# Stage boundaries with repeated reciprocals as weights, halved weight slots, and layer-norm squares added on VectorE

## The chip, the core and the metric

The kernel runs on one core of one Trainium2 chip. The metric is the device time of one execution in microseconds. Engines: TensorE (PE; its weight loads stand apart as PEld), VectorE (DVE), ScalarE (ACT), GpSimd (POOL), and SyncE (SP), which issues the transfers.

## What is computed

A trunk of two layers on x of 512 tokens and 1024 channels, float32. Each layer is a SwiGLU feed-forward block (inner width 2816) with weight 1/2, a mixer, and a second such block; every block normalises its input and its output:

```python
f = swiglu(rms_norm(h, norm_pre[i, 0]), w_ffn_in[i, 0], w_ffn_out[i, 0])
h = h + FFN_RES_WEIGHT * rms_norm(f, norm_post[i, 0])
t = rms_norm(h, norm_pre[i, 1])
...                                    # layer 0: attention; layer 1: convolution module
h = h + rms_norm(t, norm_post[i, 1])
f = swiglu(rms_norm(h, norm_pre[i, 2]), w_ffn_in[i, 1], w_ffn_out[i, 1])
h = h + FFN_RES_WEIGHT * rms_norm(f, norm_post[i, 2])

def rms_norm(x, g):
    return x * rsqrt(mean(x * x) + 1e-6) * g

def conformer_conv_module(h, ...):
    a = h @ w_pw1 + b_pw1
    u = a[..., :CONV_CH] * sigmoid(a[..., CONV_CH:])
    y = causal depthwise convolution of u, width 31, + b_dw
    mu = mean(y); var = mean((y - mu) ** 2)          # layer_norm over channels
    y = silu((y - mu) * rsqrt(var + 1e-5) * ln_g + ln_b)
    return y @ w_pw2 + b_pw2
```

## The kernel before

Everything is held transposed: channels on the 128 partitions in eight chunks, tokens on the free axis. Weights come as a stream of slots, 128 x 1024 float32 each (eight 128x128 blocks, or six for the last group of a feed-forward block), into a ring of four (`raw`). For precision each slot is split: ScalarE copies it to `w_hi` (line 745), VectorE subtracts to get `w_lo` (line 970), and each block product is three passes, hi x hi, lo x hi, hi x lo (lines 360 to 362). Slot n + 4 is split once slot n has been multiplied; its raw data was loaded by SyncE when the slot before it in the ring place had been split.

There are six sub-layers (`sub` 0 to 5). Each ends in `down`, which leaves the output f in SBUF, chunk by chunk, squares it on ScalarE and adds the squares on VectorE. The last slot of it is computed in two halves of 256 tokens (`last_slot`). Then comes the boundary. TensorE's `post_stat` sums the squares over the channels as one column of four per-token-block values (`add_columns`, line 377), ScalarE takes the root (line 757), VectorE inverts it to `r_col`, 128 x 4 (line 975), and multiplies it onto four diagonals (line 976); TensorE spreads it over all partitions with a product of ones and the diagonals (`broadcast`, line 383). Fillers (`keep_warm`, line 371) stand before and after it. VectorE then normalises f from that bank and adds the residual (lines 1069, 1074), ScalarE makes x_hi of the next sub-layer (line 749), and its first body starts (`four_slots`, line 399). The last ring place's slot is split within the boundary: ScalarE behind the root, VectorE behind the diagonals. A second inversion and spread, for the norm before the sub-layer, stands within the first body, which `r_pre` (line 762) keeps. The sixth boundary ends in `output`: TensorE adds four residual chunks (line 500) and products with the gains (line 509), VectorE the rest.

In the convolution (sub 4) TensorE runs sixteen bodies of the first projection (two for each chunk of channels), and between them `convolve(j)` (line 656) on groups of channels with their taps on a matrix that VectorE builds (line 1214). The input u of it goes through DRAM: VectorE's gate, a store (line 273) and a load in another layout (line 279), both queued on SyncE. Results are biased and centred on VectorE (lines 1226, 1232) and squared on ScalarE (line 900); the sums over channels are products with `same_q` on TensorE (line 664; 4 products of 128x128, which float32 makes eight passes). Those of the values are `sum_rest`, those of the squares `sum_squares`. The order of each engine's work is written out by hand in the code, and semaphores join them. VectorE's first step on the variance is line 1281.

## Time and profile before

| | us |
|---|---|
| median of 3 runs | 1902.97 (1902.47 to 1903.03) |
| the profiled execution | 1901.29 |
| its span | 1899.4 |
| TensorE busy | 1878.8 (99%) |
| VectorE busy | 1009.5 (53%) |
| ScalarE busy | 634.0 (33%) |

Starts in the timeline are microseconds from the span's start. A float32 or float32r product shows one row for each pass. The duration of a matmul is longer than the distance to the next, because they are pipelined: a 512-column pass lasts 0.39 and the next starts 0.23 later.

### The profile page before, as it was taken

Reading aid. Unit: us, or ns where it says so; the run is one execution under the profiler, and the core shown is the slowest. Engines: PE = TensorE matmul, PEld = TensorE weight load, DVE = VectorE, ACT = ScalarE, POOL = GpSimd, SP = SyncE. Lnnn points to the kernel's source line nnn. Section 1 sums busy time; section 2 is a strip of 40 time slices with the busy share of each in tenths; the row PEclk is TensorE's granted clock in tenths of the full one; section 3 lists DMA queues with packets and bytes.
Section 4 is the critical chain, followed back from the end, with each engine's and each line's share of the span. In section 5 each row is a group of like instructions: output and inputs, shape, how many; then the busy total and the mean of one; then the engine's idle time right before and its main releaser. Section 6 shows DMA issues by size and latency. Waiting matters only on the chain.

```text
span 1899.4 us, 24198 instructions
## 1 busy us (share of the span) xinstructions
PE 1878.8 (99%) x8969; PEld 1543.8 (81%) x8969; DVE 1009.5 (53%) x1377; ACT 634.0 (33%) x915; POOL 28.0 (1%) x54
## 2 busy tenths in 40 slices
PE   8999999999999999999999999999999999999998
PEld 6888888887688888888788888887998888888886
DVE  5534434688666434435754443457765674344345
ACT  5322322346634223223442232234112543222223
POOL 0000000021000000000000000000000000000000
PEclk9999999999999999999999999999999999999999
DMA  5333233321023332333233323332332223332331
GB/s 189 111 100 100 88 102 98 114 87 58 24 77 100 100 99 89 100 100 100 67 122 100 99 89 100 100 111 80 122 121 79 78 82 95 100 100 91 97 99 56
DMA packets 62096, 181.49 MB, mean 96 GB/s; under 512 B 7088, under 2 KB 16448, under 8 KB 62032
## 3 DMA queue, kind: packets, MB, share of 16 engines
q1 hardware_dynamic: 60432, 179.09, 29.7%
q0 software_dynamic: 1600, 1.51, 0.3%
q8 instruction: 44, 0.72, 0.2%
q14 instruction: 20, 0.16, 0.0%
HBM read 173.63 MB, written 6.29 MB: 95 GB/s over the span
## 4 chain that ended last, share of the span: by engine, by line
PE 96%; DVE 3%; ACT 1%; DMA 0%; issue 0%; SPq 0%; DVEq 0%; ACTq 0%
PE bank L360 27%; PE bank L362 27%; PE bank L361 27%; PE bank L656 3%; PE bank L399 2%; PE bank L400 2%; PE bank L403 2%; PE bank L377 1%; PE bank L605 1%; PE bank L589 1%; PE bank L664 1%; DVE w_lo L970 1%; PE bank L570 1%; ACT w_hi L745 0%; DVE h_resid L1074 0%; PE bank L546 0%
## 5 line engine op out<-in xcount | busy, mean ns | idle before, releaser
L970 DVE TENSOR_TENSOR w_lo<-w_raw,w_hi 128x1024 fp32r<-128x1024 f32 x312 | 381.5, 1225 | 447.5 <-ACT w_hi L745 436.8
L360 PE MATMUL bank<-x_hi,w_hi 128*128 128x512 f32 x1448 | 567.6, 392 | 0.8 <-DVE gate_tmp L1003 0.2
L362 PE MATMUL bank<-x_hi,w_lo 128*128 128x512 f32 x1448 | 563.5, 389 | 0.0
L361 PE MATMUL bank<-x_lo,w_hi 128*128 128x512 f32 x1448 | 563.4, 389 | 0.0
L745 ACT ACTIVATE w_hi<-w_raw 128x1024 fp32r<-128x1024 f32 x312 | 328.2, 1055 | 602.0 <-PE bank L362 600.0
L360 PE MATMUL bank<-a_hi,w_hi 128*128 128x512 f32 (+1 forms) x844 | 320.7, 380 | 0.4 <-DVE w_lo L970 0.4
L360 PEld LDWEIGHTS bank<-x_hi,w_hi 128*128 128x128 f32 x1448 | 271.9, 188 | 60.2 <-issue 2.6
L361 PE MATMUL bank<-a_lo,w_hi 128*128 128x512 f32 (+1 forms) x844 | 319.9, 379 | 0.0
L362 PE MATMUL bank<-a_hi,w_lo 128*128 128x512 f32 (+1 forms) x844 | 319.9, 379 | 0.0
L361 PEld LDWEIGHTS bank<-x_lo,w_hi 128*128 128x128 f32 x1448 | 271.9, 188 | 57.2 <-issue 1.4
L362 PEld LDWEIGHTS bank<-x_hi,w_lo 128*128 128x128 f32 x1448 | 271.9, 188 | 56.5
L360 PEld LDWEIGHTS bank<-a_hi,w_hi 128*128 128x128 f32 x844 | 158.8, 188 | 32.0 <-DVE a_lo L1015 1.0
L362 PEld LDWEIGHTS bank<-a_hi,w_lo 128*128 128x128 f32 x844 | 158.8, 188 | 29.8
L361 PEld LDWEIGHTS bank<-a_lo,w_hi 128*128 128x128 f32 x844 | 158.8, 188 | 29.7
L1003 DVE TENSOR_TENSOR up_tmp<-bank,r_pre 128x512 f32<-128x512 f32 x96 | 66.2, 690 | 191.7 <-PE bank L362 191.7
L776 ACT ACTIVATE a_hi<-up_tmp 128x512 f32 (+1 forms) x88 | 55.6, 632 | 276.6 <-DVE up_tmp L1013 276.6
L774 ACT ACTIVATE gate_tmp<-gate_tmp 128x512 f32<-128x512 f32 x88 | 55.7, 632 | 160.4 <-DVE gate_tmp L1003 160.4
L1015 DVE TENSOR_TENSOR a_lo<-up_tmp,a_hi 128x512 f32 (+1 forms) x88 | 60.9, 692 | 79.9 <-ACT a_hi L776 79.9
L399 PE MATMUL bank<-x_hi,w_hi 128*128 128x512 f32 x168 | 67.2, 400 | 9.0 <-DVE w_lo L1319 8.2
L1003 DVE TENSOR_TENSOR gate_tmp<-bank,r_pre 128x512 f32<-128x512 f32 x106 | 72.4, 683 | 0.0
L1013 DVE TENSOR_TENSOR up_tmp<-up_tmp,gate_tmp 128x512 f32<-128x512 f32 x88 | 60.9, 692 | 13.7 <-ACT gate_tmp L774 3.3
L400 PE MATMUL bank<-x_hi,w_lo 128*128 128x512 f32 x168 | 66.4, 395 | 0.0
(169 smaller groups left out, 1263.4 us busy)
## 6 DMA issues: line engine op xcount, KB each, us to landing
w_raw<-stream SPq DMA_DIRECT2D x312, 512.0 KB, 3.5
h_resid<-xT SPq DMA_DIRECT2D x8, 256.0 KB, 6.5
w_raw<-stream SPq DMA_DIRECT2D x8, 256.0 KB, 6.1
u_scratch<-V SPq DMA_DIRECT2D x8, 256.0 KB, 2.3
u_groups<-u_scratch SPq DMA_DIRECT2D x8, 256.0 KB, 2.7
qT<-z_scratch SPq DMA_DIRECT2D x8, 256.0 KB, 3.7
outT<-h_resid SPq DMA_DIRECT2D x8, 256.0 KB, 2.2
z_scratch<-kT SPq DMA_DIRECT2D x4, 256.0 KB, 2.5
```

The source lines that it names most:

```text
L360: nc.tensor.matmul(out, lw[0], lx[0], start=first, stop=False)
L361: nc.tensor.matmul(out, lw[0], lx[1], start=False, stop=False)
L362: return nc.tensor.matmul(out, lw[1], lx[0], start=False, stop=last)
L399: nc.tensor.matmul(bank[s][:, :], blk(w_hi, s, k), x[0][:, k, :], start=(k == 0), stop=False)
L400: nc.tensor.matmul(bank[s][:, :], blk(w_lo, s, k), x[0][:, k, :], start=False, stop=False)
L656: last = nc.tensor.matmul(bank[6 + j % 2][:, g * NT:(g + 1) * NT], mats[g][:, m, :, :].rearrange("p c q -> p (c q)"), ug[:, j % 2, g, m:m ...
L745: nc.scalar.activation(w_hi[:, s, :], raw[:, s, :], ACT.Copy).then_inc(s_hi, 1)
L774: nc.scalar.activation(g, g, ACT.Silu).then_inc(s_act, 1)
L970: nc.vector.tensor_tensor(w_lo[:, s, :], raw[:, s, :], w_hi[:, s, :].bitcast(F32), ALU.subtract).then_inc(s_lo, 1)
L1003: nc.vector.tensor_tensor(dst, bank[s][:, :], r_pre[:, :], ALU.mult).then_inc(s_evac, 1)
L1013: nc.vector.tensor_tensor(U[:, p, :], U[:, p, :], G[:, p, :], ALU.mult).then_inc(s_prod, 1)
L1015: nc.vector.tensor_tensor(a_lo[:, chunk, :], U[:, p, :], a_hi[:, chunk, :].bitcast(F32), ALU.subtract).then_inc(s_a, 1)
```

## The change

The diagonals are gone. `broadcast` multiplies with the column of `r_col`, repeated 128 times, as the weights, and the identity as the moving data, one product of 128x128 for each of four token blocks. Since it reads `ident`, the first spread waits for the constants. The fillers before it are three instead of six. In the last slot's turn both halves of the weights of the last ring place are split on their own: on ScalarE around the second square, ahead of the root; on VectorE one before the reciprocal, one after. The sum of the layer norm's squares is made by seven additions on VectorE, and TensorE sums one tile instead of eight.

```diff
             def broadcast():
-                return nc.tensor.matmul(BCAST[:, :], ones[:, :], sq[:, 0, :],
-                                        start=True, stop=True)
+                for t in range(NB):
+                    ins = nc.tensor.matmul(BCAST[:, t * P:(t + 1) * P], r_col[:, t:t + 1].broadcast_to([P, P]),
+                                           ident[:, :], start=True, stop=True)
+                return ins
...
                 else:
-                    keep_warm(6)
+                    keep_warm(3)
...
-                def sum_squares(j):
-                    if j == 0:
-                        pe.wait_ge(s_root, 2 * sub + 1)
-                    pe.wait_ge(s_zsq, j + 1)
-                    sum_groups(STAT, zsq[j % 3], j == 0, j == KD - 1).then_inc(s_sqmm, 1)
+                def sum_squares():
+                    pe.wait_ge(s_root, 2 * sub + 1)
+                    pe.wait_ge(s_zsqadd, KD - 1)
+                    sum_groups(STAT, zsq_sum, True, True).then_inc(s_sqmm, 1)
...
                         nc.scalar.activation(sq[:, m % 2, HALVES[0]], f[:, m, HALVES[0]], ACT.Square
                                              ).then_inc(s_fsq0, 1)
+                        if n + RING < SLOTS:
+                            act.wait_ge(s_raw[s], 16 * (n // RING) + 32)
+                            act.wait_ge(s_mm, n + 1)
+                            nc.scalar.activation(w_hi[:, s, W_HALVES[0]], raw[:, s, W_HALVES[0]], ACT.Copy
+                                                 ).then_inc(s_hi_half, 1)
                         act.wait_ge(s_evac, n + 1)
                         nc.scalar.activation(sq[:, m % 2, HALVES[1]], f[:, m, HALVES[1]], ACT.Square
                                              ).then_inc(s_fsq, 1)
+                        if n + RING < SLOTS:
+                            nc.scalar.activation(w_hi[:, s, W_HALVES[1]], raw[:, s, W_HALVES[1]], ACT.Copy
+                                                 ).then_inc(s_hi, 1)
...
-                link(nc.vector.reciprocal(r_col[:, :], root_col[:, :]))
-                nc.vector.tensor_tensor(diag, ident[:, None, :].broadcast_to([P, NB, P]),
-                                        r_col[:, :, None].broadcast_to([P, NB, P]), ALU.mult).then_inc(done, 1)
+            def inverse_of_roots(done):
+
+                nc.vector.reciprocal(r_col[:, :], root_col[:, :]).then_inc(done, 1)
...
+                def add_squares(j):
+                    dve.wait_ge(s_zsq, j + 1)
+                    if j >= 2:
+                        dve.wait_ge(s_zsqadd, j - 1)
+                    nc.vector.tensor_tensor(zsq_sum, zsq_sum, zsq[j % 2], ALU.add).then_inc(s_zsqadd, 1)
```

VectorE's queue at the boundary of sub 0. f_out<-bank3 is the last evacuation, w_lo the low half of a weight slot, f_out<-f_out,bank5 the first normalisation. Before:

```order
L1024 TENSOR_TENSOR f_out<-bank3,f_out 128x256
L975 RECIPROCAL r_col<-root_col 128x4
L976 TENSOR_TENSOR sq_tmp<-ident,r_col 128x512
L970 TENSOR_TENSOR w_lo<-w_raw,w_hi 128x1024
L1069 TENSOR_TENSOR f_out<-f_out,bank5 128x512
```

and in the changed kernel:

```order
L1034 TENSOR_TENSOR f_out<-bank3,f_out 128x256
L982 TENSOR_TENSOR w_lo<-w_raw,w_hi 128x512
L987 RECIPROCAL r_col<-root_col 128x4
L982 TENSOR_TENSOR w_lo<-w_raw,w_hi 128x512
L1083 TENSOR_TENSOR f_out<-f_out,bank5 128x512
```

The diagonals left the queue, and half of the weight slot stands before the reciprocal.

ScalarE's queue at the same place; sq_tmp are the squares, root_col the root, x_hi the next sub-layer's input. Before:

```order
L795 ACTIVATE sq_tmp<-f_out 128x256
L798 ACTIVATE sq_tmp<-f_out 128x256
L757 ACTIVATE root_col<-bank4,eps 128x4
L745 ACTIVATE w_hi<-w_raw 128x1024
L749 ACTIVATE x_hi<-h_resid,cols 128x512
```

and in the changed kernel:

```order
L795 ACTIVATE sq_tmp<-f_out 128x256
L800 ACTIVATE w_hi<-w_raw 128x512
L803 ACTIVATE sq_tmp<-f_out 128x256
L806 ACTIVATE w_hi<-w_raw 128x512
L757 ACTIVATE root_col<-bank4,eps 128x4
L749 ACTIVATE x_hi<-h_resid,cols 128x512
```

The slot's copy moved from behind the root to before it, in two parts.

TensorE's queue at the end of the convolution, from convolve(6) on: bank67 takes the convolution, bank5 the sums of the values, bank4 those of the squares. Before:

```order
L656 MATMUL bank67<-u_groups,f_out 128x128 x27
L656 MATMUL bank67<-u_groups,tap_matrix 128x128 x9
L664 MATMUL bank5<-kT,conv_consts 128x128 x8
L664 MATMUL bank4<-gate_tmp,conv_consts 128x128 x4
L664 MATMUL bank4<-up_tmp,conv_consts 128x128 x4
L664 MATMUL bank4<-sum_sq,conv_consts 128x128 x4
L656 MATMUL bank67<-u_groups,f_out 128x128 x27
L656 MATMUL bank67<-u_groups,tap_matrix 128x128 x9
L664 MATMUL bank5<-rope_cos,conv_consts 128x128 x4
L664 MATMUL bank5<-rope_sin,conv_consts 128x128 x4
L664 MATMUL bank4<-gate_tmp,conv_consts 128x128 x4
L664 MATMUL bank4<-up_tmp,conv_consts 128x128 x4
```

and in the changed kernel:

```order
L662 MATMUL bank67<-u_groups,f_out 128x128 x27
L662 MATMUL bank67<-u_groups,tap_matrix 128x128 x9
L670 MATMUL bank5<-kT,conv_consts 128x128 x8
L662 MATMUL bank67<-u_groups,f_out 128x128 x27
L662 MATMUL bank67<-u_groups,tap_matrix 128x128 x9
L670 MATMUL bank5<-rope_cos,conv_consts 128x128 x4
L670 MATMUL bank5<-rope_sin,conv_consts 128x128 x4
L670 MATMUL bank4<-gate_tmp,conv_consts 128x128 x4
```

Three of the sums of squares stood between the two convolutions and two at the end (three more before the last body); one is left, at the end. On VectorE the additions 1 and 2 stand ahead of the bias of group 6, 3 to 5 behind its centring, 6 and 7 behind that of group 7.

## Rows read from the trace of the kernel before

**Rows 1.** The page's part 4, the chain that ended last, by engine.

```profile
PE 96%; DVE 3%; ACT 1%; DMA 0%; issue 0%; SPq 0%; DVEq 0%; ACTq 0%
```

**Rows 2.** Timeline, all engines, boundary of sub 0: start us, us, engine, line, out<-in.

```profile
373.71 0.42 DVE L1024 TENSOR_TENSOR f_out<-bank,f_out 128x256 f32<-128x256 f32 x1 [0.60 <-PE bank L362]
374.17 0.42 ACT L798 ACTIVATE sq_tmp<-f_out 128x256 f32<-128x256 f32 x1 [1.68 <-DVE f_out L1024]
...
374.32 1.03 PE L377 MATMUL bank<-ones,sq_tmp 128*128 128x1 f32 x8
...
375.22 1.46 PE L371 MATMUL bank<-mask,ident_b 128*128 128x512 bf16 x6
375.39 0.26 ACT L757 ACTIVATE root_col<-bank,eps 128x4 f32<-128x4 f32 x1 [0.81 <-PE bank L377]
...
375.69 0.18 DVE L975 RECIPROCAL r_col<-root_col 128x4 f32<-128x4 f32 x1 [1.55 <-ACT root_col L757]
375.90 0.69 DVE L976 TENSOR_TENSOR sq_tmp<-ident,r_col 128x512 f32<-128x512 f32 x1
376.63 1.23 DVE L970 TENSOR_TENSOR w_lo<-w_raw,w_hi 128x1024 fp32r<-128x1024 f32 x1
...
376.65 1.12 PE L383 MATMUL bank<-sq_tmp,ones 128*128 128x512 f32 x2
...
377.61 2.32 PE L371 MATMUL bank<-mask,ident_b 128*128 128x512 bf16 x10
...
377.81 0.69 DVE L1069 TENSOR_TENSOR f_out<-f_out,bank 128x512 f32<-128x512 f32 x1
...
380.09 0.50 PE L399 MATMUL bank<-x_hi,w_hi 128*128 128x512 f32 x1 [0.16 <-ACT x_hi L749]
```

**Rows 3.** Timeline, TensorE, end of the convolution.

```profile
1429.14 1.06 PE L664 MATMUL bank<-gate_tmp,conv_consts 128*128 128x128 f32 x8
...
1437.28 6.19 PE L656 MATMUL bank<-u_groups,f_out 128*128 128x128 f32 x54
...
1445.31 1.95 PE L664 MATMUL bank<-kT,conv_consts 128*128 128x128 f32 x16
...
1449.78 6.19 PE L656 MATMUL bank<-u_groups,f_out 128*128 128x128 f32 x54
...
1461.38 1.06 PE L664 MATMUL bank<-up_tmp,conv_consts 128*128 128x128 f32 x8
```

**Rows 4.** Timeline, VectorE, end of the convolution.

```profile
1458.02 0.69 DVE L1226 TENSOR_TENSOR rope_sin<-bank,conv_consts 128x512 f32<-128x512 f32 x1 [9.27 <-PE bank L656]
...
1460.69 0.29 DVE L1276 TENSOR_SCALAR mean_rest<-bank 128x128 f32<-128x128 f32 x1 [1.25 <-PE bank L664]
...
1462.55 0.29 DVE L1281 SCALAR_TENSOR_TENSOR var<-bank,mean_early 128x128 f32<-128x128 f32 x1 [0.65 <-PE bank L664]
```

**Rows 5.** Groups by line: shapes, count, busy us, mean ns, idle before.

```profile
L1319 DVE TENSOR_TENSOR w_lo<-w_raw,w_hi 128x512 fp32r<-128x512 f32 x8 | 5.4, 692 | 1.9 <-ACT w_hi L939 1.9
...
L939 ACT ACTIVATE w_hi<-w_raw 128x512 fp32r<-128x512 f32 x8 | 5.0, 630 | 1.6 <-DMA w_raw<-stream 1.4
```

**Rows 6.** Timeline, TensorE, last boundary.

```profile
1885.06 1.10 PE L500 MATMUL bank<-h_resid,ident 128*128 128x512 f32 x2
1886.48 1.13 PE L383 MATMUL bank<-sq_tmp,ones 128*128 128x512 f32 x2 [0.32 <-DVE sq_tmp L976]
```

**Rows 7.** Timeline, SyncE's queue, and the landing of the transfer at 1445.70.

```profile
1442.47 0.32 SPq L273 DMA_DIRECT2D u_scratch<-V  x1
...
1445.70 0.37 SPq L279 DMA_DIRECT2D u_groups<-u_scratch  x1
...
DMA to landing us min/median/max: 2.8/2.8/2.8
```

**Rows 8.** Timeline, TensorE, the program's first passes.

```profile
11.76 1.91 PE L403 MATMUL bank<-x_lo,w_hi 128*128 128x512 f32 x4
...
15.41 1.07 PE L403 MATMUL bank<-x_lo,w_hi 128*128 128x512 f32 x4
```

More of the change, by code:

```diff
@@ L148, in build_program @@
         zg = [z.rearrange("p (g n) -> p g n", g=GROUPS) for z in (kf[:, 0:T], kf[:, T:2 * T], rc[:, :], rs[:, :])]
-        zsq = [z.rearrange("p (g n) -> p g n", g=GROUPS) for z in (G[:, 0, :], U[:, 0, :], ss[:, :])]
+        zsq_sum, *zsq = [z.rearrange("p (g n) -> p g n", g=GROUPS) for z in (G[:, 0, :], U[:, 0, :], ss[:, :])]
         m0, dl, var = sb("mean_early", [P, NT]), sb("mean_rest", [P, NT]), sb("var", [P, NT])
@@ L422, in spread @@
                 def spread():
+                    if sub == 0:
+                        pe.wait_ge(s_const, CONSTS)
                     pe.wait_ge(s_diag, 2 * sub + 1)
@@ L696, in convolution @@
                 convolve(5)
-                for j in range(3):
-                    sum_squares(j)
                 body(n0 + 15, 3)
@@ L702, in convolution @@
                     sum_rest(j)
-                for j in range(3, 6):
-                    sum_squares(j)
                 convolve(7)
@@ L707, in convolution @@
                     sum_rest(j)
-                for j in range(6, 8):
-                    sum_squares(j)
+                sum_squares()
             def layer_norm():
@@ L971, in next_slot, with half_slot @@
                                         ).then_inc(s_lo, 1)
-            def on_diagonals(done):
-                link(nc.vector.reciprocal(r_col[:, :], root_col[:, :]))
-                nc.vector.tensor_tensor(diag, ident[:, None, :].broadcast_to([P, NB, P]),
-                                        r_col[:, :, None].broadcast_to([P, NB, P]), ALU.mult).then_inc(done, 1)
+            def half_slot(s, at):
+                return nc.vector.tensor_tensor(w_lo[:, s, at], raw[:, s, at], w_hi[:, s, at].bitcast(F32),
+                                               ALU.subtract)
+            def inverse_of_roots(done):
+                nc.vector.reciprocal(r_col[:, :], root_col[:, :]).then_inc(done, 1)
             def invert(count):
@@ L1057, in down @@
                         to_f(s, m, how, HALVES[1]).then_inc(s_evac, 1)
+                        if n + RING < SLOTS:
+                            dve.wait_ge(s_hi_half, last_of + 1)
+                            half_slot(s, W_HALVES[0])
                     if n + RING < SLOTS and m < KD - 2:
@@ L1064, in boundary @@
                 if sub < SUBS - 1:
-                    next_slot(n0 - 1, RING - 1)
+                    dve.wait_ge(s_hi, n0 + RING)
+                    half_slot(RING - 1, W_HALVES[1]).then_inc(s_lo, 1)
                 dve.wait_ge(s_bc, 2 * sub + 2)
@@ L1269, in conv @@
                 matrices(7)
-                for i in (6, 7):
-                    biased(i)
-                    centre(i)
+                add_squares(1)
+                add_squares(2)
+                biased(6)
+                centre(6)
+                for i in (3, 4, 5):
+                    add_squares(i)
+                biased(7)
+                centre(7)
+                add_squares(6)
+                add_squares(7)
                 dve.wait_ge(s_dlmm, KD - EARLY)
```

13 lines of the change are left out of this document (7 added, 6 removed).

## The prediction

> **What bounds the kernel now.** I read the page's chain of waits first, then the timeline around the first stage boundary, then the end of the convolution, then the end of the program. The chain is TensorE for 96% [rows 1], so a change gains only where TensorE stands idle, runs fillers, or does passes that are taken away. Such places are the five boundaries between stages, the convolution's passes that add squares, and the last few microseconds.
>
> At a boundary [rows 2] the last half of f leaves its bank at 373.71, ScalarE squares it at 374.17, TensorE's column sums (its last row starts at 374.32) end and ScalarE's root starts at 375.39. Then VectorE inverts (375.69), multiplies onto the diagonal (375.90 to 376.59), TensorE spreads it from 376.65, and the first normalisation starts at 377.81. The first real matmul follows at 380.09, after 0.16 of idle time that x_hi ends; the fillers at 375.22 and 377.61 occupy TensorE meanwhile. At 377.81 two things end together: the spread, 1.16 after its start, and w_lo's 1.23 from 376.63, since VectorE works in order. Taking only the diagonal away would leave w_lo, whose w_hi ScalarE copies behind the root. So the two edits need each other.
>
> **The boundary's edits.** (1) The diagonal product, 0.69 and its semaphore, goes: reciprocal's end 375.87 to spread's start 376.65 is 0.78; the spread could start at 375.93 if TensorE is free. The fillers are 0.216 apart (ten from 377.61 in 2.32, the last 0.38 long), so three from 375.22 leave TensorE free at 375.87. They don't hold it.
> (2) One 512-column fp32 product (two passes, 1.16 to the reader) becomes four of 128 columns, so eight passes whose weights are one column of r_col repeated. No such weights stand in the trace. The nearest rows are the group sums, also eight fp32 passes of 128x128 onto 128 columns: 1461.38 to VectorE's 1462.55, so 1.17 [rows 3, 4]. I take 1.17. Bounds: 0.90 (only the distance of eight passes) and, if a repeated read cost twice the 0.112 of such a pass, 2.1.
> (3) The weight slot in halves. ScalarE's two 512-wide copies are 0.63 each, VectorE's halves 0.69 [rows 5]. The first copy can start when the last multiply is done, 373.73 (VectorE's evacuation starts at 373.71), and ends at 374.36; the square then starts 0.1 to 0.2 late against 374.17. TensorE's sums still have the earlier block in hand then, so 0 to 0.1 of it reaches the root. The second copy starts at about 374.7 and ends by 375.4 or a little sooner, at the root's old start: another 0 to 0.1. I take 0.03 together. VectorE's first half fits in its 1.55 of idle time before 375.69; the second, 375.96 to 376.65, is over before the spread, at 375.93 + 1.17 = 377.10. What is late next is therefore the spread.
> Sum: 377.81 - 377.10 - 0.03 = 0.68. VectorE, x_hi and the first matmul move together: the ten later fillers then end near 379.1, x_hi at 379.40. From there the first body is a TensorE stream as before. Five boundaries with the same pattern: 5 x 0.68 = **3.4**, between 1.5 (0.3 each, if the copies take both bounds and the spread is 0.2 longer) and 3.6.
> The other spread in each first body and at the start stands inside a TensorE stream: about 0.91 of passes before, 8 x 0.112 = 0.90 now. VectorE's diagonal there was done before TensorE came to it. I take nothing, within 0.1 each way for the six.
>
> **The last boundary** has no slots to convert. There two add_residual passes start at 1885.06 and the spread at 1886.48, 0.32 after they let go, for the diagonal [rows 6]. The two long passes hold TensorE about 0.96, as the spread's own two do from 376.65 to 377.61. So the spread can start near 1886.02 and the gain is **0.45**; at most 0.7. All that follows hangs on VectorE to the end.
>
> **The convolution.** Eight groups of sum_squares passes, 0.895 each (1429.14 is the first, 1461.38 the last; 40 passes from 1445.31 to 1449.78 give 0.112 each) [rows 3], become one. Three stand before the last body, three before the last convolve, two at the end.
> First three: TensorE goes from one stream to the next without idle time, so 24 x 0.112 = **2.68** is gained in full; weights and banks of the next body are ready long before.
> Next three, 2.68 again: but everything that feeds convolve(7) hangs on the body before convolve(6). Before: convolve(6) starts at 1437.28, the u store goes out at 1442.47, the load of its groups at 1445.70, and it lands 2.8 later, at 1448.50 [rows 7], hidden until 1449.78. This is 11.22 behind convolve(6)'s start. TensorE's work in between was 12.50 and is now 12.50 - 2.68 = 9.82. It will wait 11.22 - 9.82 = 1.40, and 0.05 for the semaphore: the gain is **1.23**. The bound below is 0.5 (both transfers 0.35 slower), above 2.0 (0.35 faster). The load is queued on SyncE behind a store and a y load, as before, and nothing in that queue gets later.
> This is where a page speaks against the rows. The Trainium skill, DMA: Bandwidth & Descriptors, Anatomy of one DMA, has a transfer cost about 2 us and its bytes over 436 GB/s; that makes 2.6 for each 256 KB, 5.2 for store and load where the rows show 3.2 and 2.8. By the page the wait would be 0.6 and the gain 2.0; the row decides.
> VectorE's seven added sums are 0.69 each, 4.8 in all. Five fall into its 9.27 of idle time before 1458.02 [rows 4] and cost nothing; without this cover they would cost 3.4. Two follow the last centring, which ends at 0.73 + 0.69 behind 1458.02, at 1459.44. Then ScalarE's square (0.63) ends at 1460.10, the sum 1460.14 to 1460.83, one group of passes from 1460.88, and its reader at +1.17: 1462.05 instead of 1462.55. The three steps on the mean, from 1460.69 to 1461.90 before, slip by about 0.1 and end by 1462.0. So **0.50**, between 0.2 and 0.7.
> Sum of the convolution: 2.68 + 1.23 + 0.50 = 4.4.
>
> **The sum:** 3.4 + 0.45 + 4.4 = 8.25. The profiled execution took 1901.29 (span 1899.4), so 1893.0 there; the median of the runs is 1.7 higher, so 1902.97 - 8.25 = 1894.7.
>
> **Rivals.** *A, no wait in the convolution:* the transfers land sooner than in the rows, and 1.45 more is gained: 1893.3. For it: the u load was hidden before, so nothing tested its latest moment. Against: store and load keep the same neighbours on SyncE, and both were measured. Chance 0.08.
> *B, the wait in the convolution eats the second gain and the half slots sit on the boundary's path:* 1.23 and 5 x 0.38 less, 1897.8. For it: ScalarE has four steps between the evacuation and the root where it had one. Against: its steps fit by the sum above. Chance 0.10.
> *C, repeated weights read slowly:* 12 spreads have 96 passes, all on TensorE's path. From 0.086 more each on (8.25 / 96) nothing is gained; at twice the 0.112 it is 96 x 0.112 = 10.8, so 1905.5, slower than before. For it: no row shows such a read. Against: ones and ident blocks in the same array pass at 0.112, whatever their content. Chance 0.04.
> *D, the clock falls at the boundaries:* three fillers fewer each time, and a new idle stretch of 1.4 in the convolution. After the idle start of the trace four passes take 1.91 at 11.76, and the same four 1.07 at 15.41 [rows 8]: the 1.2 GHz level by their distance, though the granted clock of the page reads 0.9 or more there, then the 2.4 GHz level. The slow episode was twelve passes, 12 x (1.91 - 1.07) / 4 = 2.5. Five of them: 12.5, so 1894.7 + 12.5 = 1907.2, slower. It decides from four falls on. For it: the fillers exist for this. Against: TensorE stays about as dense as before, because the fillers cover a stretch that is itself gone. Chance 0.04.
> Here the Trainium skill, TensorE: Matmul & The Clock Gate, What's actually happening, says that throttled is the default state and activity releases it. The trace agrees for the start; that three fillers are too few, no row shows.
> *E, not what it says:* VectorE's normalisation still waits for weights, because the second half comes late. It would lose the boundaries' 3.4 and keep the rest: 1898.1. Chance 0.04.
>
> **How the numbers follow.** The forecast, 1893.5 to 1896.5 by its own terms, has 0.70. The range of 1892.8 to 1898.2 takes in A, B and E. A measurement of this kernel can tell about 0.2%, 3.8 us, from no change; faster means under 1899.2. Forecast, A, B and E all lie there; I move 0.05 of them to the middle, where their bounds add up, and C and D are shared between the middle and slower. Faster 0.87, same 0.07, slower 0.06.
>
> **What would show it.** Right: at each boundary the reciprocal's end to the normalisation's start falls from 1.94 to about 1.23 and VectorE's last half slot ends before the spread; TensorE idle for 1.4 before the last convolve, ended by the u_groups load; the variance's first step 4.2 behind the end of convolve(7) instead of 4.7; the spread's eight passes 0.112 apart; passes 0.23 apart right behind every boundary. Wrong: passes wider apart (C), boundary passes twice as far apart (D), a w_lo half that ends last (E), a root that starts more than 1.8 behind the evacuation (B), no idle time before convolve(7) (A).

## The result, and the profile after

| | before | changed |
|---|---|---|
| median of the runs | 1902.72 (1901.01 to 1903.03, 4) | 1891.55 (1890.96 to 1891.99, 4) |
| the profiled execution | 1901.29 | 1891.92 |
| its span | 1899.4 | 1890.0 |

The ratio is 0.9947, with a 95% interval of 0.9935 to 0.9958. The kernel is faster, as forecast, by more than the 0.2% that can be told. But 1891.55 lies 1.25 below the range of 1892.8 to 1898.2, and 3.15 below the forecast of 1894.7.

The page of the changed kernel, parts 1 and 4. TensorE is busy for 9.7 less than before, and the span is 9.49 shorter (1899.45 and 1889.96, with one digit more than the page prints); the chain is TensorE's as in [rows 1].

```profile
PE 1869.1 (99%) x8970; PEld 1542.6 (82%) x8970; DVE 1005.7 (53%) x1377; ACT 634.6 (34%) x920; POOL 28.0 (1%) x54
...
PE 96%; DVE 2%; ACT 1%; DMA 1%; issue 0%; SPq 0%; DVEq 0%; ACTq 0%
```

The boundary of sub 0 in the changed kernel, timeline of all engines, to lay beside [rows 2]:

```profile
373.57 0.42 DVE L1034 TENSOR_TENSOR f_out<-bank,f_out 128x256 f32<-128x256 f32 x1 [0.60 <-PE bank L364]
373.63 0.63 ACT L800 ACTIVATE w_hi<-w_raw 128x512 fp32r<-128x512 f32 x1 [1.28 <-PE bank L364]
...
374.17 0.40 ACT L803 ACTIVATE sq_tmp<-f_out 128x256 f32<-128x256 f32 x1
...
374.47 0.61 ACT L806 ACTIVATE w_hi<-w_raw 128x512 fp32r<-128x512 f32 x1
...
375.09 0.81 PE L373 MATMUL bank<-mask,ident_b 128*128 128x512 bf16 x3
375.26 0.26 ACT L757 ACTIVATE root_col<-bank,eps 128x4 f32<-128x4 f32 x1 [0.17 <-PE bank L379]
...
375.56 0.18 DVE L987 RECIPROCAL r_col<-root_col 128x4 f32<-128x4 f32 x1 [0.57 <-ACT root_col L757]
375.65 0.66 DVE L982 TENSOR_TENSOR w_lo<-w_raw,w_hi 128x512 fp32r<-128x512 f32 x1
...
375.79 1.16 PE L386 MATMUL bank<-ident,r_col 128*128 128x128 f32 x8
...
376.78 2.32 PE L373 MATMUL bank<-mask,ident_b 128*128 128x512 bf16 x10
376.99 0.69 DVE L1083 TENSOR_TENSOR f_out<-f_out,bank 128x512 f32<-128x512 f32 x1 [0.67 <-PE bank L386]
...
379.27 0.50 PE L403 MATMUL bank<-x_hi,w_hi 128*128 128x512 f32 x1 [0.16 <-ACT x_hi L749]
```

From the reciprocal's end (375.74) to the normalisation (376.99) it takes 1.25, where it took 1.94. The normalisation now waits for the spread alone: VectorE's last half slot is over at 376.31, and VectorE then idles 0.67 until the bank is ready. The spread begins 0.05 behind the reciprocal's end. From its start to the normalisation it takes 1.20, where the one long product took 1.16. ScalarE's four steps all fit: the root still comes 1.69 behind the evacuation, as before (1.68 in [rows 2]), and ScalarE idles 0.17 ahead of it.

The end of the convolution in the changed kernel: TensorE, then VectorE, then SyncE's queue and the landing of the load at 1438.89; to lay beside [rows 3, 4, 7].

```profile
1431.70 6.19 PE L662 MATMUL bank<-u_groups,f_out 128*128 128x128 f32 x54
...
1439.74 1.95 PE L670 MATMUL bank<-kT,conv_consts 128*128 128x128 f32 x16
1441.80 6.29 PE L662 MATMUL bank<-u_groups,f_out 128*128 128x128 f32 x54
...
1453.10 1.13 PE L670 MATMUL bank<-gate_tmp,conv_consts 128*128 128x128 f32 x8 [0.33 <-DVE gate_tmp L1253]
```

```profile
1450.14 0.69 DVE L1240 TENSOR_TENSOR rope_sin<-bank,conv_consts 128x512 f32<-128x512 f32 x1 [3.38 <-PE bank L662]
...
1452.26 0.69 DVE L1253 TENSOR_TENSOR gate_tmp<-gate_tmp,sum_sq 128x512 f32<-128x512 f32 x1
...
1454.34 0.29 DVE L1307 SCALAR_TENSOR_TENSOR var<-bank,mean_early 128x128 f32<-128x128 f32 x1 [0.26 <-PE bank L670]
```

```profile
1436.88 0.32 SPq L275 DMA_DIRECT2D u_scratch<-V  x1
...
1438.89 0.37 SPq L281 DMA_DIRECT2D u_groups<-u_scratch  x1
```

```profile
DMA to landing us min/median/max: 2.9/2.9/2.9
```

Sixteen sum passes, 0.112 apart, from 1439.74 let TensorE go at 1441.53; convolve(7) starts at 1441.80. So it waited 0.27, not 1.40. The nearer reason stands in SyncE's queue: the load went out 2.01 behind the store, where [rows 7] have 3.23.

The time of an instruction that both kernels have tells where the time went. Each line is the gain since the line before it; starts of VectorE's reciprocals where not said otherwise.

| stretch | gain | forecast |
|---|---|---|
| up to the first boundary | 0.13 | 0 |
| five boundaries | 0.68, 0.74, 0.69, 0.69, 0.71: 3.51 | 3.4 |
| convolution, up to the start of convolve(6) (1437.28, now 1431.70) | 2.72 | 2.68 |
| up to the start of convolve(7) (1449.78, now 1441.80) | 2.40 | 1.23 |
| from there to var, the variance's first step (1462.55, now 1454.34) | 0.23 | 0.50 |
| from var to the reciprocal behind it | 0.05 | 0 |
| last boundary | 0.56 | 0.45 |
| all bodies between, and the end | -0.11 | 0 |
| sum | 9.49 | 8.25 |

The first row is the least steady one: in the fourteen traces taken after the one of the kernel before it lies between -0.83 and 1.01, and nearly all of that stands already at the first reciprocal of all (32.16 in the kernel before), ahead of everything that was changed.

### The profile page after: what moved, and what is told of

Its sections match the earlier page's. It is cut to its first block, busy times and chain, and to the rows that moved or that the text cites. A ratio compares the mean times of both kernels' runs of the same rounds, so it can differ in the third digit from the quotient of the medians.

```text
span 1890.0 us, 24212 instructions
## 1 busy us (share of the span) xinstructions
PE 1869.1 (99%) x8970; PEld 1542.6 (82%) x8970; DVE 1005.7 (53%) x1377; ACT 634.6 (34%) x920; POOL 28.0 (1%) x54
## 3 DMA queue, kind: packets, MB, share of 16 engines
HBM read 173.63 MB, written 6.29 MB: 95 GB/s over the span
## 4 chain that ended last, share of the span: by engine, by line
PE 96%; DVE 2%; ACT 1%; DMA 1%; issue 0%; SPq 0%; DVEq 0%; ACTq 0%
PE bank L362 27%; PE bank L364 27%; PE bank L363 27%; PE bank L662 3%; PE bank L403 3%; PE bank L404 2%; PE bank L407 2%; PE bank L379 1%; PE bank L611 1%; PE bank L595 1%; PE bank L386 1%; PE bank L576 1%; DVE h_resid L1088 0%; DVE f_out L1083 0%; PE bank L552 0%
## 5 line engine op out<-in xcount | busy, mean ns | idle before, releaser
L977 DVE TENSOR_TENSOR w_lo<-w_raw,w_hi 128x1024 fp32r<-128x1024 f32 x307 | 375.3, 1225 | 449.0 <-ACT w_hi L745 438.6
L745 ACT ACTIVATE w_hi<-w_raw 128x1024 fp32r<-128x1024 f32 x307 | 322.9, 1055 | 598.8 <-PE bank L364 596.8
```

Source lines behind the costliest of these rows:

```text
L745: nc.scalar.activation(w_hi[:, s, :], raw[:, s, :], ACT.Copy).then_inc(s_hi, 1)
L977: nc.vector.tensor_tensor(w_lo[:, s, :], raw[:, s, :], w_hi[:, s, :].bitcast(F32), ALU.subtract).then_inc(s_lo, 1)
```

## The experiments

Each kernel was timed beside the kernel before on the same chip. Its medians in four groups of runs were 1901.39 (23 executions), 1901.6 (20), 1902.06 (10) and 1901.42 (9). One kernel's executions differ by up to 2 either way, so trace differences carry the sizes and medians the verdicts.

**1. The changed kernel again, and its parts.** Three kernels ran beside it. "Boundary only" sums the squares as before:

```diff
-                sum_squares()
+                for j in range(6, 8):
+                    sum_squares(j)
...
-                add_squares(1)
-                add_squares(2)
-                biased(6)
-                centre(6)
...
+                for i in (6, 7):
+                    biased(i)
+                    centre(i)
```

"Squares only" is the kernel before with the change in the convolution alone. "No halves" has all of the change but the split weight slot, whose two copies go back to their place, whole:

```diff
-                            nc.scalar.activation(w_hi[:, s, W_HALVES[0]], raw[:, s, W_HALVES[0]], ACT.Copy
-                                                 ).then_inc(s_hi_half, 1)
...
-                            nc.scalar.activation(w_hi[:, s, W_HALVES[1]], raw[:, s, W_HALVES[1]], ACT.Copy
-                                                 ).then_inc(s_hi, 1)
...
+                next_slot(n0 - 1, RING - 1, n0 // RING - 1)
                 for k in range(KD):
                     act.wait_ge(s_h, KD * sub + k + 1)
...
-                            dve.wait_ge(s_hi_half, last_of + 1)
-                            half_slot(s, W_HALVES[0])
...
-                    dve.wait_ge(s_hi, n0 + RING)
-                    half_slot(RING - 1, W_HALVES[1]).then_inc(s_lo, 1)
+                    next_slot(n0 - 1, RING - 1)
```

> The changed kernel unaltered, to settle its size and to look a second time at the convolution's last transfers. If the one profiled trace tells the whole gain (span 1899.4 to 1890.0), it is 9.4 us faster than before, a ratio of 0.9951. If the medians so far do (1902.72 to 1891.55), it is 11.2 us, 0.9941, and 1.8 us would lie outside what the two traces show. In the trace: the u store before the last convolve landed 3.2 after its issue in the kernel before and 2.0 in the changed one. If that is an accident of one execution, it should vary between 2.0 and 3.2 here and the idle time before convolve(7) with it (0.27 to 1.45); if it is a property of the new order, it is 2.0 again.

> The changed kernel with the sums of squares put back on TensorE as eight groups of products: the boundary's edits alone. Theory (the edits are independent, each boundary worth 0.70, the last 0.55): 5 x 0.70 + 0.55 = 4.1 us faster than before, so about 1898.6 beside 1902.7. Rival (the convolution's gain needs the earlier boundary, or the boundaries give more than the trace shows): more than 5 us or less than 3. In the trace the convolution's end must look as before: convolve(7) 12.5 behind convolve(6).

> The kernel before with the squares added on VectorE and nothing else changed (diagonals, six fillers, whole last slot behind the root). Theory: the convolution gains 5.3 us as in the changed kernel (2.7 before the last body, 2.3 before the last convolve, 0.3 at the end), so about 1897.4 beside 1902.7; with a slow u store (3.2) only 4.1. Together with the boundary-only kernel the two gains should add up to the whole one within 0.5 us. Rival: they overlap, and the sum of the two is clearly more or less than the whole.

> The changed kernel with the last ring place's slot split whole, ScalarE behind the root and VectorE behind the reciprocal, as before. Theory (the two edits need each other): the normalisation at five boundaries starts when w_lo ends, as before, 0.7 later than in the changed kernel; 5 x 0.7 = 3.5 us slower than it, about 1895.1. VectorE's timeline then shows the reciprocal, about 0.8 idle for w_hi, w_lo 1.23, then the normalisation; TensorE's spread is over before that. Rival (the diagonals alone carry the boundary's gain): within 0.5 us of the changed kernel.

Measured:

| kernel | median | ratio to before | five boundaries | convolution |
|---|---|---|---|---|
| changed | 1891.68 | 0.9947 [0.9933, 0.9961] | 3.53 | 5.22 |
| boundary only | 1896.75 | 0.9977 [0.9968, 0.9986] | 3.42 | 0.00 |
| squares only | 1897.43 | 0.9979 [0.997, 0.9989] | 0.06 | 4.37 |
| no halves | 1894.97 | 0.9966 [0.9954, 0.9977] | 0.24 | 5.36 |

(The last two columns are gains in the traces, summed from reciprocal to reciprocal as above.) The parts add up: boundary only is 4.64 below the 1901.39 of the kernel before beside it, squares only 3.96, together 8.6, the changed kernel 9.7. The remaining 1.1 has one place in the traces: in squares only the load before convolve(7) landed late (its row is in experiment 4), and its convolution gained 1.0 less than in the first trace of the changed kernel.

Without the halves the boundaries' gain is nearly gone (0.24 in all), though the diagonals are, too. VectorE's queue at the boundary of sub 0 in "no halves":

```profile
375.47 0.18 DVE L980 RECIPROCAL r_col<-root_col 128x4 f32<-128x4 f32 x1 [1.55 <-ACT root_col L757]
376.42 1.23 DVE L970 TENSOR_TENSOR w_lo<-w_raw,w_hi 128x1024 fp32r<-128x1024 f32 x1 [0.77 <-ACT w_hi L745]
377.56 0.68 DVE L1072 TENSOR_TENSOR f_out<-f_out,bank 128x512 f32<-128x512 f32 x1
```

The whole slot's w_lo waits for ScalarE's copy, and the normalisation comes 1.91 behind the reciprocal's end, as before (1.94), with the spread done at 376.86.

**2. Halves only:** the changed kernel with the diagonals, the single spread and six fillers put back. The change in the convolution stays in.

```diff
+                link(nc.vector.reciprocal(r_col[:, :], root_col[:, :]))
+                nc.vector.tensor_tensor(diag, ident[:, None, :].broadcast_to([P, NB, P]),
+                                        r_col[:, :, None].broadcast_to([P, NB, P]), ALU.mult).then_inc(done, 1)
```

> The changed kernel with the diagonals and the single 512-column spread back (and six fillers): the weight slot in halves alone, at the boundaries. Theory (the two edits need each other): the spread again ends 1.16 behind the diagonals, at the same place as before; nothing is gained at the five boundaries, and the last one loses its 0.55. So 5 x 0.7 + 0.55 = 4.1 us slower than the changed kernel, about 1895.6. Rival (the half slots carry the gain): within 0.5 us of the changed kernel.

Measured: 1897.04, 0.9976 [0.9966, 0.9985]. In the trace the five boundaries gain 0.05 in all, the convolution 4.01. VectorE at the boundary of sub 0:

```profile
375.40 0.18 DVE L986 RECIPROCAL r_col<-root_col 128x4 f32<-128x4 f32 x1 [0.57 <-ACT root_col L756]
375.61 0.69 DVE L987 TENSOR_TENSOR sq_tmp<-ident,r_col 128x512 f32<-128x512 f32 x1
376.22 0.68 DVE L981 TENSOR_TENSOR w_lo<-w_raw,w_hi 128x512 fp32r<-128x512 f32 x1
377.52 0.69 DVE L1084 TENSOR_TENSOR f_out<-f_out,bank 128x512 f32<-128x512 f32 x1 [0.62 <-PE bank L386]
```

1.94 again, now with 0.62 of idle time that the late spread ends. So the two edits do need each other: either alone leaves the other chain last.

**3. Fillers.** Four kernels, each one number away from the changed one (the first two blocks of fillers at a boundary: three, and ten behind the spread):

```diff
-                    keep_warm(3)
+                    keep_warm(6)
```

```diff
-                    keep_warm(3)
+                    pass
```

The second of these is "no first"; "no fillers" leaves out keep_warm(10) as well; "four second" has:

```diff
-                    keep_warm(10)
+                    keep_warm(4)
```

> The changed kernel with six fillers before the spread instead of three. Theory: the fillers, 0.216 apart from 375.09, hold TensorE until 376.4, and the spread that could start at 375.79 waits: 0.6 at each of five boundaries, 3.0 us slower than the changed kernel, about 1894.6. Rival (the spread waits for the reciprocal anyway): no difference.

> The changed kernel with no fillers at all at the five boundaries (neither the three nor the ten). It tells whether the clock is near falling there. Theory (TensorE idles 0.6 before the spread and 2.4 behind it, and nothing waits for the fillers): no change if the clock holds. Rival (D of the prediction): the passes behind the boundary are 0.43 apart for some time, at twelve such passes 2.5 us for each boundary, up to 12.5 us slower.

> The changed kernel without the three fillers before the spread; the ten behind it stay. With none at all the kernel took 1905.7, 14 us more than the changed kernel, with TensorE's granted clock at 0.50 behind the boundary. If the three are what holds the clock, most of this comes here too: the granted clock falls at the spread, and the time is 5 us or more above the changed kernel. If the ten are, the clock stays at 1.00 and the time is that of the changed kernel within 0.5 us.

> The changed kernel with four fillers behind the spread instead of ten; the three before it stay. TensorE then idles 1.7 before the first body instead of 0.4. If the ten are what holds the clock, some boundaries fall to 0.50 and the time is 2 us or more above the changed kernel; if an idle stretch of 1.7 is short enough, it is the same within 0.5 us.

Measured:

| kernel | median | ratio to before | five boundaries, gain in the trace |
|---|---|---|---|
| six and ten | 1894.19 | 0.9962 [0.9948, 0.9976] | 0.22, 0.21, 0.16, 0.22, 0.23 |
| three and ten (changed) | 1891.5 | 0.9944 [0.9931, 0.9958] | 0.68, 0.74, 0.69, 0.69, 0.71 (first trace) |
| three and four | 1893.47 | 0.9955 [0.994, 0.9971] | 0.70, 0.70, 0.67, 0.70, 0.69 |
| none and ten | 1896.45 | 0.9967 [0.9954, 0.998] | -0.49, -0.52, 0.69, 0.71, -0.56 |
| none | 1905.74 | 1.0021 [1.0012, 1.0031] | -2.90, -1.60, -2.14, -2.90, -1.72 |

With six, the fillers are in the way: they hold TensorE until the spread can only begin at 375.50, 0.64 behind the reciprocal's end, and each boundary loses 0.5 of its 0.7. So cutting three of them is a part of the gain. With none, the rival of the falling clock comes true, in a kernel that is slower than before. "No fillers", the view by stretches (length; busy us and count of PE, PEld, DVE, ACT, POOL; granted clock; DMA share, GB/s) and TensorE's timeline:

```profile
372.00:376.00 4.00, 3.76 (x34) 3.67 (x32) 2.62 (x4) 2.23 (x6) 0.18 (x1) 1.00 0.28 76
376.00:380.00 4.00, 2.07 (x8) 1.78 (x8) 2.29 (x5) 0.11 (x2) 3.33 (x1) 0.53 0.52 185
380.00:384.00 4.00, 3.28 (x8) 2.60 (x9) 3.61 (x6) 2.43 (x4) 0.00 (x0) 0.50 0.00 1
384.00:388.00 4.00, 4.00 (x14) 3.15 (x13) 4.00 (x8) 2.36 (x4) 0.00 (x0) 0.69 0.02 4
```

```profile
374.72 1.04 PE L379 MATMUL bank<-ones,sq_tmp 128*128 128x1 f32 x8
376.33 2.07 PE L386 MATMUL bank<-ident,r_col 128*128 128x128 f32 x8 [0.57 <-DVE r_col L985]
380.72 0.79 PE L403 MATMUL bank<-x_hi,w_hi 128*128 128x512 f32 x1 [2.32 <-ACT x_hi L747]
```

The granted clock reads 1.00, then 0.53 and 0.50, the 1.2 GHz level. Ahead of the fall stand the column sums (128x1) and 0.57 of idle time. The spread's eight passes take 2.07 instead of 1.16, and the body is slow until some way past 384. At the fourth boundary it is the same; at the second, third and fifth the spread still has the full clock (1.16, behind the same 0.57 of idle time), and the clock falls in the 2.32 of idle time behind it. Against the changed kernel the five boundaries cost 3.6, 2.3, 2.8, 3.6 and 2.4, 14.7 in all; the prediction's rival priced a fall at 2.5. The Trainium skill (TensorE: Matmul & The Clock Gate, What's actually happening) has activity release the clock. This trace agrees: 1.00 comes back only behind a run of the body's passes.

"No first", TensorE at the same boundary:

```profile
376.19 2.08 PE L386 MATMUL bank<-ident,r_col 128*128 128x128 f32 x8 [0.57 <-DVE r_col L987]
378.06 3.03 PE L373 MATMUL bank<-mask,ident_b 128*128 128x512 bf16 x10
380.74 0.59 PE L403 MATMUL bank<-x_hi,w_hi 128*128 128x512 f32 x1
381.17 0.40 PE L404 MATMUL bank<-x_hi,w_lo 128*128 128x512 f32 x1
381.41 0.40 PE L403 MATMUL bank<-x_hi,w_hi 128*128 128x512 f32 x1
```

The clock has fallen here too (2.08), but it comes back with the ten fillers: only the body's first pass is still 0.43 from the next, the others are 0.24 apart. That costs 1.2 at the first, second and fifth boundary against the changed kernel and nothing at the other two. There the clock did not fall, behind the same column sums and the same 0.57 of idle time, so these alone don't decide it. In "four second", the other way round, an idle stretch of 1.46 ahead of the body does no harm:

```profile
375.25 0.81 PE L373 MATMUL bank<-mask,ident_b 128*128 128x512 bf16 x3
375.96 1.16 PE L386 MATMUL bank<-ident,r_col 128*128 128x128 f32 x8
376.95 1.03 PE L373 MATMUL bank<-mask,ident_b 128*128 128x512 bf16 x4
379.44 0.50 PE L403 MATMUL bank<-x_hi,w_hi 128*128 128x512 f32 x1 [1.46 <-ACT x_hi L749]
```

So the three fillers ahead of the spread are the ones that hold the clock, and of the ten at most four were needed in this trace. Its median is 1.8 above the changed kernel's all the same. Of that, 1.2 stands in its convolution (next experiment); no row of its boundaries shows the rest, which stays open. (In the traces another 0.2 to 0.6 lies ahead of the first boundary, where kernels vary as said above.) "No first" is 4.8 above: 3.7 at its boundaries, 0.5 to 0.7 in its convolution.

**4. The wait before convolve(7).** The forecast's term that was off. "y later" issues the y load of group 5, which stands between store and load in SyncE's queue, behind the load:

```diff
-                if j == KD - 1:
-                    load_y(5)
                 load_groups(j)
+                if j == KD - 1:
+                    load_y(5)
```

"Other groups" takes the wait away: convolve(7) reads the u of group 6 once more, loaded ahead of the store.

```diff
+                if j == KD - 1:
+                    load_groups(j)
                 store_u(j)
...
-                sp.wait_ge(s_ud[j % 2], 16 * (j // 2 + 1))
+                src = min(j, KD - 2)
+                sp.wait_ge(s_ud[src % 2], 16 * (src // 2 + 1))
```

> The changed kernel with SyncE's y load of chunk 5 put behind the load of the last u groups instead of between the u store and that load. If the y load takes the u store's bandwidth (store 3.2 in the trace before with the y load issued 0.36 behind it), the store now lands in 2.0 every time and TensorE's wait before convolve(7) is 0.3 or less. If not, store and wait vary as in the changed kernel. The time is within 0.5 us of the changed kernel either way, since y chunk 5 is wanted much later.

> The changed kernel, but the last group of convolutions, convolve(7), reads the u of group 6 again: its load into the group layout goes out before the store of u(7), which nothing now waits for in the convolution (the output is therefore computed from wrong data for those channels, with the same work). This takes away what the last convolution waits for and leaves every instruction of TensorE. Theory now (the usual pair of store 2.0 and load 2.8 leaves a wait of 0.25): no idle time before convolve(7), and from the reciprocal at the start of the convolution to the one at its end 0.25 less than in the changed kernel, so 5.6 to 5.7 gained there against the kernel before instead of 5.4, and a median 0.2 to 0.3 lower, which can't be told in the medians. Rival, the prediction's own step (a wait of 1.4 is the usual case, and the looks at the changed kernel were lucky): the trace would again show 5.6 to 5.7, but the median would be about 1.4 lower than the changed kernel's 1891.6, so 1890.2. A second rival, that the earlier load disturbs the other transfers of the stage: idle time elsewhere on TensorE in the convolution, and less than 5.4 gained.

> The changed kernel as it is, for a comparison on the same chip with the kernel whose last convolution waits for nothing. Theory now: a wait of about 0.25 before convolve(7), median 0.2 to 0.3 above the other. Forecast's step: a wait of 1.3 to 1.4 in most executions, median 1.1 to 1.4 above the other. The look's own pair of transfers may be of either kind: 2.0 and 2.8 (wait 0.25) or 3.2 and 2.8 (wait 1.3).

Measured: y later 1891.48, 0.9949 [0.9933, 0.9966]; other groups 1891.23, 0.9944 [0.993, 0.9957]; the changed kernel beside it 1891.5, 0.9944 [0.9931, 0.9958]. Without the wait the median is 0.27 lower, and the trace gains 5.71 in the convolution, 5.33 in the changed kernel beside it. So the usual execution of the changed kernel has the short wait. With a usual wait of 1.4 the medians would have been 1.1 or more apart; they are not. The start of convolve(7) in "squares only", "four second" and "other groups", TensorE's timeline of each:

```profile
1442.68 1.95 PE L669 MATMUL bank<-kT,conv_consts 128*128 128x128 f32 x16
1445.65 1.60 PE L661 MATMUL bank<-u_groups,f_out 128*128 128x128 f32 x12 [1.03 <-DMA u_groups<-u_scratch]
```

```profile
1440.01 1.95 PE L670 MATMUL bank<-kT,conv_consts 128*128 128x128 f32 x16
1443.21 4.96 PE L662 MATMUL bank<-u_groups,f_out 128*128 128x128 f32 x42 [1.26 <-DMA u_groups<-u_scratch]
```

```profile
1439.95 1.95 PE L675 MATMUL bank<-kT,conv_consts 128*128 128x128 f32 x16
1441.73 6.19 PE L667 MATMUL bank<-u_groups,f_out 128*128 128x128 f32 x54
```

All traces of kernels with the convolution's change and the full clock there in one table, but for "tail and last" below. Store and load are from issue to landing; the gap is the start of convolve(7) minus the start of the sixteen passes before it and their 16 x 0.112; the gain is from reciprocal to reciprocal. The last column is for what follows the table: where a packet of 16 KB of another queue stands.

| kernel | store | load | gap before convolve(7) | gain in the convolution | 16 KB packet |
|---|---|---|---|---|---|
| changed, three traces | 2.0 | 2.9, 3.0, 2.9 | 0.27, 0.38, 0.27 | 5.40, 5.22, 5.33 | ahead of both |
| no halves | 2.1 | 2.8 | 0.27 | 5.36 | ahead of both |
| six fillers | 2.0 | 2.8 | 0.18 | 5.41 | ahead of both |
| y later | 2.3 | 2.8 | 0.51 | 5.08 | ahead of both |
| squares only | 2.0 | 3.8 | 1.18 | 4.37 | in the load |
| halves only | 2.0 | 4.2 | 1.57 | 4.01 | in the load |
| four second | 3.2 | 2.8 | 1.41 | 4.22 | in the store |
| no first | 2.8 | 2.8 | 0.95 | 4.68 | in the store |
| no fillers | 2.0 | 2.9 | 0.32 | 5.20 | from 0.5 before the load's landing |
| other groups | - | - | 0 | 5.71 | in its early load |

Gap and gain add up to 5.5 to 5.7 in every row. "Four second" drew the very pair of [rows 7], 3.2 and 2.8, and its gap of 1.41 is the forecast's 1.40; between the starts of convolve(6) and convolve(7) it gained 1.26, where the forecast had 1.23. So the mechanism and its arithmetic hold; what was wrong is which pair the changed kernel has.

What makes a store or load take 1 longer isn't the y load between them: moved away, the pair was 5.1, and with it 4.8 to 5.0 in the changed kernel. The traces point to something else. DMA traffic within the store of the kernel before (1442.47 to 1445.68), then within that of the changed kernel (1436.88 to 1438.88): queue and kind, packets, MB, share of the 16 DMA engines:

```profile
q1 hardware_dynamic: 315, 0.59, 59.1%
q8 instruction: 1, 0.02, 1.8%
```

```profile
q1 hardware_dynamic: 204, 0.41, 66.9%
```

In the slow store stands one packet of 16 KB on the queue `q8 instruction`. It lasts 0.93, from 1443.26; the others named in the table last 0.93 to 1.41. A transfer lands in sixteen parts. In this store fifteen of them had landed by 1.99 behind the issue, as in the fast ones, and the sixteenth came at 3.21. "Four second" (1.99, then 3.18), "no first" (2.00, 2.77) and the loads of "squares only" (2.85, 3.77) and "halves only" (2.83, 4.16) look the same. So the slow transfers are those of which one part is late, beside such a packet. Over all 15 traces, 26 of 120 u stores overlap one; they took 2.8 to 5.7, 3.6 at the median, and the 94 others 2.0 at the median. (Some of these took up to 5.6; why was not followed up.) For loads the overlap isn't enough: 22 of 27 took 3.1 or less with one.

The packet's place goes with the kernel. In the three traces of the changed kernel it starts 2.0 to 2.3 ahead of the store, and in squares only and halves only 1.1 behind the load's issue. The medians agree: these two, with ten executions each, gained 3.96 and 4.56, near the 4.4 and 4.3 of their late traces and about a microsecond short of what the short gap would give, and all four executions of "four second" (1892.46 and up) lie above all of the changed kernel (1892.11 at most in 14). No run moved the packet and nothing else, so it is the likely cause, not a shown one.

**5. Towards a better version:** two edits on the changed kernel. The seventh addition goes, because TensorE sums zsq_sum (groups 0 to 6) while VectorE is still centring group 7, and then the last squares on their own. And at the last boundary the two residual passes move behind the spread.

```diff
-                for j in range(6, 8):
-                    sum_rest(j)
-                sum_squares()
+                sum_rest(6)
+                sum_squares(False)
+                sum_rest(7)
+                sum_squares(True)
...
-                    pe.wait_ge(s_evac, SLOTS)
-                    add_residual(0, 1)
...
-                add_residual(1, PE_OUT)
+                pe.wait_ge(s_evac, SLOTS)
+                add_residual(0, PE_OUT)
```

> The changed kernel with two more moves, to see whether it can be beaten. First, at the end of the convolution VectorE adds squares 1 to 6 only (6 before the bias of group 7), TensorE sums that tile between sum_rest(6) and sum_rest(7), and sums the last square itself behind sum_rest(7): the last addition (0.69 and a semaphore) leaves the chain, one group of passes (0.9) enters it, partly in 0.61 of idle time. Theory: the variance's first step comes 3.9 behind the end of convolve(7) instead of 4.4, so 0.5 faster. Second, at the last boundary the first residual product moves behind the spread, and three fillers stand there: the spread starts when the reciprocal is done, 0.2 to 0.3 earlier. Together 0.7 faster than the changed kernel, about 1890.9. Rival (the shift passes to TensorE's residual products, which end 0.6 later and then set the output): the last boundary gains nothing or loses up to 0.4, and the whole is within 0.2 of the changed kernel.

Measured: 1892.07, 0.9947 [0.9934, 0.9961], no better than the changed kernel, where 0.7 had been expected. In the trace the convolution gained 5.72, 0.3 more: its tail is 0.27 shorter, the rest is a shorter gap before convolve(7), 0.14 with a load of 2.7. At the end the spread came earlier, but not the end of the program. TensorE at the last boundary, "tail and last" first, the changed kernel second:

```profile
1877.42 1.16 PE L386 MATMUL bank<-ident,r_col 128*128 128x128 f32 x8
...
1881.85 3.60 PE L512 MATMUL bank<-f_out,gate_tmp 128*128 128x512 f32 x8
```

```profile
1877.06 1.05 PE L386 MATMUL bank<-ident,r_col 128*128 128x128 f32 x8
...
1880.53 3.60 PE L515 MATMUL bank<-f_out,gate_tmp 128*128 128x512 f32 x8
```

Its reciprocals are at 1877.18 and 1876.59. Counted from these, the spread starts at 0.24 instead of 0.47, but the gain products at 4.67 instead of 3.94: the two residual passes had stood in a gap and now stand on TensorE's path, and the end comes 0.7 later (14.12 behind the reciprocal instead of 13.41). The prediction, too, took VectorE for the bound there; this run shows TensorE's products.

## Why the prediction was right, and where it was wrong

**Right, by its own steps.** The boundary: 0.68 forecast for each, 0.68 to 0.74 measured. Spread, halves and root behaved as summed: 1.20 from the spread's start to its reader (1.17 forecast), nothing for ScalarE's copies on the root's path (0.03 forecast). Repeated weights are no slower, so rival C is out. Rival B's second part and rival E are out by the same rows. Experiments 1 and 2 show that both edits are needed, as the first section of the prediction said, and experiment 3 that the three dropped fillers are needed too, which the prediction had as a condition that the fillers "don't hold" TensorE. Rival D is real, at fewer fillers than these: three suffice, none doesn't. The first three groups of squares gave 2.72 (2.68 forecast).

**The step that failed: "this is 11.22 behind convolve(6)'s start ... it will wait 1.40 ... the gain is 1.23".** The 11.22 was taken from one execution of another kernel, whose u store took 3.2. Now convolve(7) starts 10.10 behind convolve(6) (1431.70 to 1441.80). The chain lost 1.2 at the store (2.01 from store to load instead of 3.23) and kept the load (2.9). The gain is 2.40. That sample was a slow one: a packet of the queue `q8 instruction` stands in its store and none in the changed kernel's (experiment 4). "Boundary only", whose convolution is the old one, has a pair of 2.0 and 2.8. The prediction's bounds, 0.35 either way for each transfer, were not drawn from any spread of samples. Rival A had the right case, no wait or nearly, at a chance of 0.08.

The Trainium skill (DMA: Bandwidth & Descriptors, Anatomy of one DMA) gave the prediction an estimate of 2.6 for each transfer, so a wait of 0.6 and a gain of 2.0. The section fits that sum to transfers issued through GpSimd, and these are SyncE's, which the prediction didn't say. The measured pair is 2.0 and 2.9, the wait 0.27 and the gain 2.40, so the estimate's 5.2 for the pair was nearer to the usual 4.9 than the one sample of 6.0 that the prediction let decide.

**Smaller terms.** The tail gave 0.23 instead of 0.50. On the engines it is 0.33; another 0.10 goes to the first pass behind the wait, which makes convolve(7)'s 54 passes take 6.29 instead of 6.19. VectorE's second addition waits for ScalarE's square and starts at 1452.26, 2.12 behind the bias of group 7, as summed (2.12 in the forecast). But it is TensorE that comes late: its products start 0.15 behind the end of the addition at 1452.95, and var follows 1.24 behind their start, where 0.05 and 1.17 were taken. The last boundary gave 0.56 instead of 0.45: the spread starts 0.47 behind the reciprocal's start, as forecast (0.49), and its reader follows after 1.09 instead of 1.17.

**The base, the other term that failed.** Of the 3.15 by which the forecast was too high, only 1.12 is in these terms (9.37 between the profiled executions, 8.25 forecast). It also added the 1.7 by which the median of three runs (1902.97) lay above the profiled execution. That was an accident of three runs: 62 later executions of the kernel before, in four groups, have medians of 1901.4 to 1902.1, so the profiled 1901.29 was a usual one, and the changed kernel's median lies 0.4 below its profiled execution. 1.12 between the profiled executions (1893.04 forecast, 1891.92), 1.68 from the base and 0.37 from the last make the 3.17. Taken from the profiled execution the forecast would have been 1893.0, with the term as wrong as it was. The range, moved by the same 1.68, would have begun at 1891.1 and held the measured time. The direction and its chance were not touched by either.

## What to carry to other kernels

Where a chain of two engines ends in one instruction, find both chains that end there; each edit here alone was worth next to nothing at the boundary, and a filler too many took back most of the gain. A wait that was hidden before has been seen through one pair of transfers only: look at the same kind of transfer elsewhere in the trace, and at what else is on the DMA engines at that moment, before giving it a value, and keep the base of the forecast on the execution whose rows make up the sum when the few other runs lie to one side of it.

## What the runs showed of the hardware

- float32 passes whose weights are one column of 128x1, repeated 128 times, cost the same as others: at the full clock they are 0.112 apart, like the group sums of 128x128. Eight took 1.05 to 1.16, and 2.07 at the halved clock.
- The same 256 KB store took 2.0 to 2.3 in most traces, 3.2 in two (the kernel before and "four second"), 2.8 in "no first" and 3.4 in "other groups", where the load goes out ahead of it. The load in the other layout took 2.7 to 3.0 in most, 3.8 and 4.2 in two kernels, and 4.9 in "other groups". One slow transfer of these moves the kernel by up to 1.2. But for "other groups", in each slow one a 16 KB packet of the queue `q8 instruction` (0.93 to 1.41 long) overlapped the transfer, and one of its sixteen parts landed 0.8 to 1.3 behind the other fifteen.
- Without the three fillers, behind column sums of 128x1 and 0.57 of idle time, the clock fell at the first, second and fifth boundary and stayed at the other two. Without any it fell at all five, at three of them only in the 2.32 of idle time behind the spread. With three bf16 fillers in that place (0.81) it read 1.00 at all five, even with 1.46 of idle time a little later.
